# Moving the start of the SBUF buffers of a hybrid decoder layer from 672 to 0 modulo 1024 bytes

## The reference, cut to what matters

```python
def hybrid_layer(x, ...):                       # x (1, 2048, 1024) float32
    h = rms_norm(x, norm_pre)
    proj = h @ w_in                             # 1024 -> 10,768 columns
    (z, xbc, dt_raw, q, k, v, g_attn, u, b_sc, c_sc, g_sc, merge) = split(proj)
    y_ssm  = ssd_branch(z, xbc, dt_raw, ...)    # 16 heads, chunks of 128 tokens; y = y + xs * d_skip
    y_attn = attention_branch(q, k, v) * silu(g_attn)   # windows 128/1, 512/4, 2048/16
    y_sc   = b_sc * conv3(c_sc * u) * silu(g_sc)
    gates  = sigmoid(merge)
    merged = gates[0]*(y_ssm @ p_ssm) + gates[1]*(y_attn @ p_attn) + gates[2]*(y_sc @ p_sc)
    return x + rms_norm(merged @ w_out, norm_post)
```

## The kernel before

| buffers | address before, mod 1024 (mod 128) |
|---|---|
| ident | 128 (0) |
| work, spare, keep, h_kept, raw, w_hi, w_lo, v_all, v_tri | 672 (32) |
| p_ops, p_rawb, p_sums, p_stage; s_xtok to s_btok, s_sums, s_xdt | 736 (96) |
| p_dtw | 480 (96) |
| s_cbm, s_fall, s_mix | 992 (96) |
| b_raw, b_ylo_ssd, key_hi, key_lo, att_all | 672 (32) |
| a_q, a_vruns, a_vt, b_yhi, b_ylo, o_x, o_wpost, o_sq | 160 (32) |
| a_scores, a_probs, a_probst, a_att | 544 (32) |
| o_y | 256 (0) |

## Time and profile before

### The profile page before, as it was taken

The page is one execution under the profiler, slowest core; times in us unless marked ns, Lnnn a source line. Parts: engine busy times, 40 slices in busy tenths (PEclk is TensorE's granted clock), DMA queues, the critical chain, the costliest instruction groups (busy, mean ns, idle before and its releaser), DMA issues. The chain is left out here.

```text
span 2891.4 us, 40604 instructions
## 1 busy us (share of the span) xinstructions
PE 2801.9 (97%) x14222; PEld 2373.8 (82%) x14222; DVE 1599.6 (55%) x2525; ACT 1240.7 (43%) x2258; POOL 1584.3 (55%) x1078
## 2 busy tenths in 40 slices
PE   6999999999999999999999999999999988999998
PEld 5888888888877888888887888888999967888787
DVE  6335235896534346875425555555766675853433
ACT  5232234333224443332324555555766754542332
POOL 7677778877877688777764444452111244422000
PEclk8999999999999999999999999999999989999999
DMA  4657346532225356332235555554566388865543
GB/s 124 154 155 229 114 131 165 127 111 87 73 81 189 102 165 143 103 102 73 88 110 177 166 166 156 174 171 153 176 193 173 104 248 258 276 215 164 177 152 109
DMA packets 462802, 436.06 MB, mean 151 GB/s; under 512 B 60736, under 2 KB 403008, under 8 KB 454976
## 3 DMA queue, kind: packets, MB, share of 16 engines
q1 hardware_dynamic: 460352, 425.79, 49.3%
q0 software_dynamic: 2304, 8.39, 0.7%
HBM read 290.99 MB, written 143.13 MB: 150 GB/s over the span
## 5 line engine op out<-in xcount | busy, mean ns | idle before, releaser
L531 PE MATMUL p_acc<-h_kept,w_hi 128*128 128x512 f32 x1216 | 477.4, 393 | 4.9 <-ACT work L577 3.2
L533 PE MATMUL p_acc<-h_kept,w_lo 128*128 128x512 f32 x1216 | 475.5, 391 | 0.0
L532 PE MATMUL p_acc<-h_kept,w_hi 128*128 128x512 f32 x1216 | 474.2, 390 | 0.0
L417 POOL TENSOR_TENSOR w_lo<-p_sums,w_hi 128x512 fp32r<-128x512 f32 x300 | 394.2, 1329 | 135.8 <-ACT w_hi L618 135.8
L618 ACT ACTIVATE w_hi<-p_sums 128x512 fp32r<-128x512 f32 x300 | 189.4, 632 | 476.9 <-PE p_acc L533 452.1
L531 PEld LDWEIGHTS p_acc<-h_kept,w_hi 128*128 128x128 f32 x1216 | 228.8, 188 | 54.1 <-ACT work L577 3.4
L533 PEld LDWEIGHTS p_acc<-h_kept,w_lo 128*128 128x128 f32 x1216 | 228.8, 188 | 49.8
L532 PEld LDWEIGHTS p_acc<-h_kept,w_hi 128*128 128x128 f32 x1216 | 229.0, 188 | 48.6
L531 PE MATMUL p_acc<-p_ops,w_hi 128*128 128x512 f32 x608 | 242.2, 398 | 7.1 <-DVE p_ops L719 7.1
L533 PE MATMUL p_acc<-p_ops,w_lo 128*128 128x512 f32 x608 | 239.7, 394 | 0.0
L532 PE MATMUL p_acc<-p_ops,w_hi 128*128 128x512 f32 x608 | 238.0, 392 | 0.0
(11 more groups left out here) (343 smaller groups left out, 6802.7 us busy)
## 6 DMA issues: line engine op xcount, KB each, us to landing
raw<-w_in SPq DMA_DIRECT2D x100, 512.0 KB, 5.0
s_qs<-p_stage SPq DMA_DIRECT2D x96, 256.0 KB, 4.0
work<-s_gates SPq DMA_DIRECT2D x48, 512.0 KB, 7.4
p_rawb<-w_in SPq DMA_DIRECT2D x38, 512.0 KB, 3.8
keep<-w_in SPq DMA_DIRECT2D x38, 512.0 KB, 5.1
s_xbc<-p_stage SPq DMA_DIRECT2D x32, 512.0 KB, 2.6
work<-s_xbc SPq DMA_DIRECT2D x16, 1024.0 KB, 7.1
spare<-s_qs SPq DMA_DIRECT2D x16, 1024.0 KB, 5.7
```

The lines of the kernel that those rows point to most:

```text
L417: tt(w_lo[:, k], weight(u, k), w_hi[:, k], ALU.subtract).then_inc(w_made, 1)
L531: pe.matmul(bank, hi, ops[k][:, 0, c], start=c == 0, stop=False)
L532: pe.matmul(bank, hi, ops[k][:, 1, c], start=False, stop=False)
L533: last = pe.matmul(bank, lo, ops[k][:, 0, c], start=False, stop=c == 3)
```

## The change

The skip weights move from behind v_ones to behind eps, and an unused buffer of 72 floats follows them: 17,056 + 64 + 288 = 17,408 = 17 x 1024. Everything from work to v_ones then lies 352 bytes higher. p_ops and all that shares its place lie 288 bytes higher, since the 64 bytes of v_dskip no longer stand before them. The buffers of the attention, merge and output stages lie 352 bytes higher. Modulo 1024 the three large groups of the table are then at 0, 0 and 0 (b_raw to att_all) and 512 (a_q and the others); s_cbm, s_fall and s_mix are at 256, a_scores to a_att at 896, p_dtw at 768 and o_y at 608. Modulo 128 all of them are at 0, but o_y at 96. ident stays where it is. No instruction, wait, transfer or order is changed.

```diff
         ident = s.sb("ident", [P, P])
         eps = s.sb("eps", [P, 1])
+        dskip = s.sb("dskip", [P, HEADS])
+        s.sb("to_a_kilobyte", [P, 72])
         work, spare, keep = s.sb("work", [P, 2, SEQ]), s.sb("spare", [P, 2 * SEQ], F32R), s.sb("keep", [P, HALF])
...
-            v.update({"tri": k.sb("v_tri", [P, P]),
-                      "ones": k.sb("v_ones", [P, P]), "dskip": k.sb("v_dskip", [P, HEADS])})
+            v.update({"tri": k.sb("v_tri", [P, P]), "ones": k.sb("v_ones", [P, P]), "dskip": dskip})
```

## The result

| what | before | after |
|---|---|---|
| median (lowest to highest, runs) | 2898.05 us (2885.67 to 2908.17, 6) | 2876.03 us (2871.69 to 2879.6, 6) |
| ratio of the two, 95% interval | | 0.9936 (0.9915 to 0.9956) |
| span of the profiled execution | 2891.4 us | 2870.1 us |
| time of the profiled execution | | 2871.69 us |

By the medians the gain is 22 us (the quotient of the two is 0.9924), by the ratio on record, 0.9936, it is 18.6 us of 2898; either is well above the 8.9 us that were forecast. An execution's own time is only 1.6 us above its span. The 7.9 us that I set between span and median were mostly the spread between executions, so the comparison goes by spans and by the ratio.

A forecast was written before the change was run, and what follows sets the result against it. The prediction took TensorE's matmul pace to bound the kernel, busy 97% of the span. Only the projection's 8.9 us counted, all other terms 0: 2899.3 - 8.9 = 2890.4 us, range 2885 to 2903.

The forecast's parts named there:

- The projection's term: Projection: with p_ops in step with the weights, each set falls 0.12 us; over 74 sets 8.9 us.
- The step: Projection, p_ops against the weights: simultaneous SBUF reads disturb each other at addresses differing by 64 modulo 128; 8.9 us gained.
- Other engines and transfers: GpSimd's low part and the transfers: new addresses change nothing that reaches the end; taken as 0.
- that 22%: Projection: GpSimd, next in load, is busy 78% of TensorE's busy time; changes within the remainder were to move no end.
- More than forecast: Rival: SSD stage's gate products also come into step, 8.9 + 2.9 = 11.8 us gained, 2887 us; chance 0.06.
- Slower: Rival: common start at 0 is itself bad, every float32r pair takes p_ops' pace; +10 us, 2909 us; chance 0.13.
- The transposes: Transposes with ident: rival that equal remainders cost 3 ns each, losing 4.3 us, 2894.7 us; chance 0.10.
- Nothing happens: Rival, projection: p_ops is slow for a reason other than its remainder, such as its SBUF region; 2899.3 us; chance 0.21.

The follow-up runs named there:

- e1: The kernel before, unchanged, profiled and timed once more: 2906.39 us, ratio 1.0004.
- e3: The changed kernel with 64 unused bytes ahead of p_ops, so p_ops and its neighbours alone are off: 2888.94 us, ratio 0.9942 to before.
- e2: The kernel before with 64 unused bytes ahead of p_ops, bringing it to the weights' remainder modulo 128: 2907.88 us, ratio 1.0010.
- e4: The changed kernel with 32 bytes of padding in place of 288, large buffers at 768 modulo 1024: 2874.09 us, ratio 0.9905 to before.
- e7: The changed kernel with 96 bytes of padding, large buffers at 832 modulo 1024: 2893.40 us, ratio 0.9948 to before.
- e10: The changed kernel with 160 bytes of padding, large buffers at 896 modulo 1024: 2891.91 us, ratio 0.9959 to before.
- e12: The changed kernel with raw alone moved to 160 modulo 256: 2876.87 us, ratio 0.9909 to before.
- e8: The kernel before, addresses unchanged, with three waits keeping GpSimd's low parts off VectorE's addition and scalings in the scan stage: 2879.00 us, ratio 0.9905.
- the six traces: Traces without added waits and with all large buffers off a multiple of 256: before, e1, e2, e5, e7, e10; scan stage 463.8 us in the mean.
- the five: Traces without added waits and with large buffers at a multiple of 256: after, e3 (p_ops' group excepted), e4, e6, e14; scan stage 447.5 us in the mean.
- e5: The changed kernel without the padding, large buffers at 736 modulo 1024: 2896.26 us, ratio 0.9967 to before.
- e6: The changed kernel with 256 unused bytes ahead of p_ops: 2885.89 us, ratio 0.9925 to before.
- e14: The changed kernel once more, no edit: 2876.38 us, ratio 0.9918 to before.
- e11: The changed kernel with keep alone moved to 160 modulo 256: 2895.15 us, ratio 0.9976 to before.
- e13: The kernel before with keep alone moved to a multiple of 256: 2890.06 us, ratio 0.9953.
- e9: The changed kernel with the three GpSimd waits of e8: 2872.26 us, ratio 0.9886 to before.
- e15: e9's kernel once more, on the same chip as e14: 2874.76 us, ratio 0.9901 to before.

## Why the prediction was wrong

**The projection's term held in size: 8.9 us forecast, 7.9 measured up to the scan stage, 9.2 between the first and last start of line 531.** The set fell by 19.16 - 19.04 = 0.12 us as forecast. The 32 sets of the earlier trace rows fell by 613.10 - 609.27 = 3.83 us, which is 0.12 each. In the traces of all kernels the scan stage begins at 1525.7 to 1530.0 us where the difference is 0 or 256, and at 1534.9 to 1543.9 us where it is 64 or 128. Product 4 had only lagged behind product 3, as the earlier trace rows had shown.

**Its reason was mis-stated.** The step said that the reads get in each other's way "when their addresses differ by 64 modulo 128". They do when the two differ by 64 or by 128 modulo 256: +0.12 us a set (e1, e3) and +0.17 (e2). They don't at 0 or 256, wherever the two begin (after, e4 to e7, e10). Other differences were not tried., which I took for "equal modulo 128", are b_yhi and b_ylo at 160 modulo 1024 and key_hi at 672, 512 apart and so equal modulo 256 as well: the row could not tell the two. Before has a difference of 64 and after one of 0, so the size came out right all the same; that was luck in part, for e2, which brings p_ops in line by the stated rule, has the slower set. The rule of the Trainium skill that I set against it (page "TensorE: Matmul & The Clock Gate", section "Step-by-step: what each phase is for", independent ports) would have made this part 0; e2 and e3 speak against it as a rule on time, since of TensorE's operands in the projection only p_ops moved there.

**The step that failed is "Other engines and transfers".** It said of transfers "a few per cent of it are under 0.5 us either way. I take 0", and the part before it that what other engines gain or lose "moves no end, as long as it stays under that 22%". Both were read from the projection, where TensorE never waits, and from the last chain. The scan stage has another limit: there VectorE's additions and scalings stand in the chain of every chunk, and TensorE did wait for them. The earlier trace rows showed it, and I read 10.4 us as small rather than ask why an operation of 480 ns kept TensorE waiting for 3.1 us. In its place the runs showed, step by step:

1. Transfers to and from buffers that begin off a multiple of 256 have longer packets: 30.6 to 31.5 ns for 512 bytes on average against 28.6 to 28.8 (e4 against e7 and e10). For stores it shows by itself: 2048 bytes out of raw take 88.5 ns against 85.5 (e12), and 256 bytes out of p_stage 18.4 ns in e3, where only p_ops' group moved, against 17.2. Loads are not exempt: with raw alone off, 17% of the 512-byte packets took over 30 ns in e12's projection, where raw is only loaded, against 2% after.
2. The weights of the scan stage land later, 7.5 to 7.6 us from their issue against 6.7 to 7.0, and the low part starts past 15.6 us of the chunk, over VectorE's addition. The held addition delays the scalings, and in every other chunk a second low part then lies over these.
3. Operations with two SBUF inputs on VectorE stand still meanwhile (up to 2419 ns in place of 1228, 2557 in place of 480), and TensorE waits. Take the overlap away, and the stage is quick with the packets as slow as ever (e8).

The measured size of the missed term is 16.4 us between the two profiled spans, and about 16 between the means of the six traces and the five (463.8 and 447.5 us); the waits give 21.9 (e1 to e8, 464.6 to 442.7 us). The ratios agree roughly: e3, with this gain alone, has 0.9942, which is 17 us. Between e5, e7 and e10, which have the projection's gain alone (0.9958 in the mean), and after, e4, e6 and e14 (0.9921) it is 11 us.

For stores, which read SBUF, the first step agrees with the Trainium skill, page "DMA: Bandwidth & Descriptors", section "How a descriptor splits into AXI transactions": a read has to start from a 256-byte aligned address, and what it fetches ahead of the first byte is not used. By that rule the change should have had an entry for stores in the prediction. Stated for reads, it doesn't account for the loads of e12. The third agrees with its page "SBUF — State Buffer", section "SBUF: two separate sides": VectorE and GpSimd take turns at a shared pair of ports when VectorE's operation has two inputs in SBUF. Here the low part, itself with two inputs, held one of VectorE's scalings up for 2557 - 480 = 2077 ns.

**The rivals.** None described this. "More than forecast" had the right sign but the wrong place: the gate products that I meant to come into step could give 2.9 us, and the scan stage was freed of pauses instead. "Slower" is refuted by products 0 and 1 at 5.44 us for the two; its premise, a start at 0 as such, by e4 and e5, which have the same pace. Its price was also worked out unevenly: 228.3 - 226.7 is 1.6 ns a matmul, and the sum took 2.2. The transposes kept their 272 ns, though ident and its partners now have the same remainder modulo 128; the row of after that answers to the last of the earlier trace rows:

```profile
L1647 PE MATMUL a_pst<-ident,a_probs x600: 269/272/328, 1985.2 to 2291.8; 128*128 128x128 f32 x150
```

So it isn't the equal remainder that costs 3 ns; the product and the transpose differ in kind. "Nothing happens" leaned on the earlier trace rows, the small p_dtw. Its pairs have other numbers after (392 ns with h_kept, 396 with p_ops, at difference 0 both), so those few matmuls don't follow the rule found here, and they were no evidence for either side.

**What stays open.** Why TensorE's two reads disturb each other by the remainder modulo 256 and not otherwise. Why the place of keep alone makes and unmakes most of the second gain in the ratios (e11, e13), and why e6 and e14, at multiples of 256, still had late weights and two long chunks each. When the target of a load matters: with raw it did (e12), with keep it didn't (e11). And the 2.9 us of the later stages, which differ from one execution to the next.

## What to carry to other kernels

Where an operation of one shape has a least and a greatest duration far apart in the rows, find what ran beside it before calling the wait on it small: here waits of 10.4 us stood for some 16 to 22 us; behind two of the three long ones the clock was lower as well. Put the buffers of transfers, and the moving and stationary operands of TensorE, at multiples of 256 bytes; 32 bytes of padding did it here. Where a transfer's landing decides which engines overlap, an explicit wait on the harmless engine makes the order certain: e9 and e15, the change with three waits, have the lowest ratios, 0.9886 and 0.9901 (the intervals overlap those of e4 and e14), and the smaller spread on either chip.

## What the runs showed of the hardware that was not expected

- A moving operand 64 or 128 bytes off its stationary partner modulo 256 costs 7 or 16 ns for three matmuls of 512 columns (687 and 696 against 680 ns by most of their triples). The lag outlives its cause by some 12 matmuls: before, the four triples of product 4 took 698, 691, 697 and 684 ns with both operands in step.
- The 512-byte packets have a median of 27 ns with either placement. What changes is a second group: 31% took 31 to 41 ns before and 1.5% after.
- The loads into a buffer at 160 modulo 256 land later (7.4 us against 6.7 to 7.0, e12's raw), though few of the scan stage's 512-byte packets are long.
- VectorE's addition took up to 3444 ns and its scaling up to 2560 in place of 1224 to 1228 and 480, while GpSimd's low part ran (e11).
- Behind two pauses in the scan stage of before TensorE's granted clock was at its lower level, 1.2 of 2.4 GHz, for 6.8 us (from 1767 us) and 3.4 us (from 1941 us). After had such a stretch only at the stage's beginning, where before has one too.
